# Rotary embedding in a two-layer encoder step: the exchange of halves made by on-chip transfers in place of permutation matmuls

## The chip, the cores and the metric

The kernel runs on one core of a Trainium2 chip. The metric is the device time of one execution in microseconds (us), as the median of the runs. Times inside the execution are read from a profile of one of them; there a time such as "at 110.98" counts from the start of the span.

## The reference

One inference step of a 2-layer encoder over 512 prompt tokens and 32 decode tokens, d_model 1024. Each layer projects the normed input with one wide matrix, feeds four head groups, merges them, and adds an MLP and a gated per-layer embedding. The change touches the rotary embedding only, which five 128-row (or narrower) tiles of a layer go through:

```python
def rope(x, pos):
    half = x.shape[-1] // 2
    ...
    x1, x2 = x[..., :half], x[..., half:]
    return jnp.concatenate([x1 * cos - x2 * sin, x2 * cos + x1 * sin], axis=-1)
...
    q_b = rope(s_q.reshape(b, t, SWA_HEADS, SWA_HEAD_DIM), pos)      # 4 heads x 64
    k_b = rope(s_k.reshape(b, t, SWA_KV_HEADS, SWA_HEAD_DIM), pos)   # 2 heads x 64
    k_pe = rope(m_kr, pos)                                           # 1 x 32
    q_p = rope(m_qr.reshape(b, t, MLA_HEADS, MLA_ROPE_DIM), pos)     # 4 heads x 32
```

## The kernel before

Activations lie feature-major: 128 features on the partitions, 544 tokens (512 + 32) along the row. So the two halves of a head are different partitions, 32 apart for heads of 64 and 16 apart for heads of 32, and the exchange of halves moves whole rows between partitions. The sign of the sine is folded into the table `sin`.

The input projection is worked off as units of 128 output features. The first 15 are, in order: MISC (with the 32 rotary key rows), Q0 Q1 K0 K1 V0 V1 (the delta rule), CKV, SK, SV, QR, SQA, SQB, Z0, Z1. TensorE makes a unit with `product` (L1821): 8 k-tiles, each in three passes, since weights and activations are split in a high part and a rest. For each unit a weight goes through SyncE (load to `raw`, 512 KB), ScalarE (`high`, L928, which first waits for the product two units back), GpSimd (`rest`, L799), and VectorE takes the product out of PSUM (`in_tile`, `evacuate`, L1331 and L1332, which links `freed`).

Between the halves of a product and after it TensorE does other work, listed in `HOOKS`: slot `2 * unit` comes in the middle of the unit, slot `2 * unit + 1` behind it. Every engine runs through the same list in its own `mid_unit`. In the middle of SK, SV, SQA, SQB and Z0 stands a rope item: R_KPE, R_SK, R_QR, R_SQA, R_SQB. In the same slots stand steps of the delta rule: `prep` (n, 0) behind a unit and (n, 1) in the middle of the next, from behind CKV to the middle of QR; then `level` (n, 0) in the middle and (n, 1) behind, from the middle of SQA on. The order inside a `prep` or `level` step matters here:

- `prep` (n, 0) ends on VectorE with L1513, which marks `prep_u`. TensorE's `prep` (n, 1) is 24 + 24 matmuls (L1930); the second 24 wait for that mark. VectorE's part of `prep` (n, 1) is `row_sources` (L1478) and L1519, L1520; TensorE's next row sums (L1957, L1958) wait for them.
- `level` (n, 0): TensorE multiplies three batches into PSUM (`xs_pe`), ScalarE copies them out (L1045, `xs`). `level` (n, 1): TensorE multiplies three batches (`ys_pe`), and its third waits until VectorE has finished the first (L1527, L1529, `td`).

A rope item works so: TensorE's `rotate` multiplies the evacuated tile `xr` by a permutation matrix into the idle PSUM bank (L1923, in `both`), marks `rotated`; VectorE's `finish_rope` multiplies that by the sine (L1364), `xr` by the cosine (L1365), and adds the two to the place where the tile is used. For QR these are four additions (L1380), one per head. TensorE waits for `roped` before the next unit's product, as that takes the bank. VectorE does `finish_rope` in the order of `HOOKS`, ahead of the delta step of its slot. `t1`, the tile named rope in the profile, is VectorE's scratch.

Of the kernel before, what the change touches and what calls it, by code (L numbers as in the profile page):

```python
# [20 lines left out]
ALU = mybir.AluOpType  # L21
# [44 lines left out]
OUTPUTS = O_PLE + 2 * KT  # L66


(K_IDENT, K_TRIBD, K_ONESBD, K_ONES, K_ROT64, K_ROT32) = (i * P for i in range(6))
K_MASK = 6 * P  # L70
K_ISTK = K_MASK + LEVELS * C
K_TRI = K_ISTK + C
K_SEL = K_TRI + C
# [189 lines left out]


R_KPE, R_SK, R_QR, R_SQA, R_SQB = range(5)


def hooks():
# [68 lines left out]
def build(nc, w_units, w_kv, params, consts, x_t, p_t, conv_state, ckv_cache, kpe_cache, k_cache, v_cache,  # L337
          s_state, sconv_state, y_t, gdn_s_p, gdn_s_s, conv_p, conv_s, swa_k_p, swa_k_s, swa_v_p, swa_v_s,
          ckv_p, ckv_s, kpe_p, kpe_s, sconv_p, sconv_s):
    with ExitStack() as ctx:  # L340
# [162 lines left out]
        c_r = signal("c_r", 1)  # L503
        c_done = signal("c_done", 1)
        rope_in = signal("rope_in_s", 4)
        rotated = signal("rotated", 5)
        roped = signal("roped", 5, 1)
        v_raw = signal("v_raw", 1)
        misc_in = signal("misc_in", 1)
# [405 lines left out]
        def _(act):  # L915
# [89 lines left out]
            def inv_rms(l, phase):  # L1005
# [2 lines left out]
                link(act, act.activation(two(rms[:]), pt[:, 0:2, 0:HALF], ACT.Ln, bias=eps, scale=1.0 / D), act_step, l)  # L1008
                mark(act.activation(rms[:], rms[:], ACT.Exp, scale=-0.5), rms_ready)

            def l2_square(l, j):

                act.wait_ge(*silud.at(l, j + 1))
                mark(act.activation(l2_scratch[j], qkv[:, j, 0:TOK], ACT.Square), qk_sq)
# [82 lines left out]

            def mid_unit(l, n):
                for item, *a in HOOKS[n]:
                    if item == "c_square":  # L1100
                        act.wait_ge(*craw.at(l, 1))
                        act.wait_ge(*l2n.at(l, 4))
                        act.activation(sqt[:, 0:SEQ], ckv[:, 0:SEQ], ACT.Square)
                        mark(act.activation(sqt[:, SEQ:TOK], ckv[:, SEQ + PAST:KEYS], ACT.Square), c_sq)
                    elif item == "c":
                        b = 2 - 2 * slot(l, n // 2)
                        act.wait_ge(*c_sum.at(l, 1))
                        link(act, act.activation(two(sqt[:]), pp[:, b:b + 2, 0:HALF], ACT.Ln, bias=eps, scale=1.0 / P),
                             act_step, l)
                        mark(act.activation(sqt[:], sqt[:], ACT.Exp, scale=-0.5), c_r)  # L1110
                    elif item == "l2_square":
                        l2_square(l, *a)
                    elif item == "delta" and a[0] != "gates":
                        step(l, *a)
# [183 lines left out]
        def _(dve):  # L1298
# [55 lines left out]
                a = sq[:, 0:2 * SEQ].rearrange("p (n r t) -> p n r t", r=2, t=C)[:, :, tile, :]  # L1354
                return [(a, slice(0, SEQ)), (sq[:, 2 * SEQ + tile * DEC:2 * SEQ + (tile + 1) * DEC], slice(SEQ, TOK))]

            def finish_rope(l, j, b):

                rows = slice(0, DEC) if j == R_KPE else slice(0, P)
                cos, sin = (cos32, sin32) if j in (R_KPE, R_QR) else (cos64, sin64)  # L1360
                src = misc if j == R_KPE else xr
                dve.wait_ge(*rotated.at(l, j + 1))
                dve.wait_ge(trig.sem, 16 * (l + 1))
                step(dve.tensor_tensor(two(t1[rows, :]), pp[rows, b:b + 2, 0:HALF], two(sin[rows, :]), ALU.mult), l)  # L1364
                step(dve.tensor_tensor(src[rows, :], src[rows, :], cos[rows, :], ALU.mult), l)  # L1365
                if j in (R_SQA, R_SQB):
                    for a, t in swa_q_parts(j - R_SQA):
                        s0, s1 = src[:, t], t1[:, t]
# [306 lines left out]
            def mid_unit(l, n):  # L1675
                for item, *a in HOOKS[n]:
# [7 lines left out]
                    elif item == "c":  # L1684

                        dve.wait_ge(*c_r.at(l, 1))
                        g = par[:, R_CNORM:R_CNORM + 1]
                        dve.scalar_tensor_tensor(ckv[:, 0:SEQ], ckv[:, 0:SEQ], g, sqt[:, 0:SEQ], ALU.mult, ALU.mult)
                        mark(dve.scalar_tensor_tensor(ckv[:, SEQ + PAST:], ckv[:, SEQ + PAST:], g, sqt[:, SEQ:TOK],
                                                      ALU.mult, ALU.mult), c_done)  # L1690
                    elif item == "rope":
                        finish_rope(l, a[0], 2 - 2 * slot(l, n // 2))
                    elif item == "delta":
                        delta(l, *a)

            dve.wait_ge(*gains_in.at(0, 16))
            for m in range(KT - 1):
# [101 lines left out]
        def _(pe):  # L1799
# [130 lines left out]
                    ins = pe.matmul(dst[r, j * C:(j + 1) * C], lhsT(r), rhs(r), start=True, stop=True)  # L1930
                return ins

            def rotate(l, j, b, slot_free):

                rows = slice(0, DEC) if j == R_KPE else slice(0, P)
                wait_apart(pe, slot_free, rope_in.at(l, j) if j else misc_in.at(l, 1))
                perm = k_(K_ROT32 if j in (R_KPE, R_QR) else K_ROT64)[rows, 0:rows.stop]
                mark(both(l, pp[rows, b:b + 2, :], perm, (xr if j else misc)[rows, :]), rotated)

            def step(l, kind, n, s):  # L1940
                n0 = n * BC
                if kind == "gates" and n == 0:
# [149 lines left out]
            def mid_unit(l, n):  # L2092
                b = 2 - 2 * slot(l, n // 2)
                for item, *a in HOOKS[n]:

                    slot_free = freed.at(l, n // 2)
                    if item == "rope":
                        rotate(l, a[0], b, slot_free)
                    elif item == "c":
                        pe.wait_ge(*slot_free)  # L2100
                        pe.wait_ge(*c_sq.at(l, 1))
                        mark(both(l, pp[:, b:b + 2, :], ones, sqt), c_sum)
# [13 lines left out]
            for l in range(DEPTH):  # L2116
                first_units(l)
                assert U_CKV > 1 and U_V0 > 1
                for u in range(2, N_PRE):
                    for item, *a in HOOKS[2 * u - 2]:  # L2120

                        if item == "rope":
                            pe.wait_ge(*roped.at(l, a[0] + 1))
                        elif item == "c":
                            pe.wait_ge(*c_r.at(l, 1))
                    product(l, u, u, ha[l], range(KT), between=lambda: mid_unit(l, 2 * u))
                    mid_unit(l, 2 * u + 1)
# [100 lines left out]
def constants(norm_final):  # L2228
# [7 lines left out]
    c[:, K_TRIBD:K_TRIBD + P] = same & (i <= j)  # L2236
    c[:, K_ONESBD:K_ONESBD + P] = same
    c[:, K_ONES:K_ONES + P] = 1
    c[:, K_ROT64:K_ROT64 + P] = (i ^ 32) == j
    c[:, K_ROT32:K_ROT32 + P] = (i ^ 16) == j  # L2240
    k = np.arange(C)[None, :]
    for lv in range(LEVELS):

# [147 lines left out]
```

## Time and profile before

| what | value |
|---|---|
| time, median of 3 runs | 1542.1 us (1542.02 to 1543.05) |
| profiled execution, its own time | 1542.11 us |
| span of its trace | 1540.3 us (so 1.8 us lie around it) |
| TensorE's granted clock over the span | 0.998 |
| TensorE matmul / weight load busy | 1508.1 us (98%) / 1430.6 us (93%) |
| VectorE / ScalarE / GpSimd busy | 997.4 / 710.2 / 832.9 us |
| mean busy share of the 16 DMA engines, in the slices of the rope items | 0.1 to 0.2 |

Busy shares are averages over the whole span. What the rope items cost must be read from their two stretches, about 72 to 142 us (layer 0) and 830 to 900 us (layer 1). The rows quoted below are of layer 0; layer 1 repeats them 757.98 us later (its R_QR matmuls start at 867.84 against 109.86) within 0.3 us.

### The profile page before, as it was taken

The page shows a single profiled execution, that of the slowest core. Times are in us where ns is not written, and L with a number is a line of the kernel's source. Part 1 is how long each engine was busy: PE and PEld are TensorE (multiplying, and loading weights), DVE is VectorE, ACT ScalarE, POOL GpSimd, SP SyncE. Part 2 cuts the span into 40 slices and gives each one's busy share as a digit, 9 for nine tenths or more (in the row PEclk, how much of TensorE's full clock was granted, in tenths as well). Part 3 has the DMA queues.
Part 4 walks back from the last instruction along what each step waited for, and adds up shares of the span by engine and source line. Part 5 has one row for each costly group of instructions (what it writes and reads, how often), then busy time and mean ns, then how long its engine had stood idle before and what let it go on. Part 6 is the DMA issues. An engine that isn't in the chain of part 4 may idle for free.

```text
span 1540.3 us, 33894 instructions
## 1 busy us (share of the span) xinstructions
PE 1508.1 (98%) x14202; PEld 1430.6 (93%) x14202; DVE 997.4 (65%) x1674; ACT 710.2 (46%) x1280; POOL 832.9 (54%) x468
## 2 busy tenths in 40 slices
PE   7999999999999999999999999999999999999997
PEld 6999888899999999999998998888999999999996
DVE  7865535547848668586688654464487594766955
ACT  6621445535434344445455224464454443434553
POOL 4354112265866849578643541114659476694973
PEclk9999999999999999999999999999999999999999
DMA  6211011332241412322322110214323224142132
GB/s 207 80 46 43 21 53 42 53 131 83 83 137 54 135 59 94 99 69 100 106 79 70 43 44 15 59 46 71 126 80 105 88 81 139 45 135 69 42 96 86
DMA packets 45129, 123.81 MB, mean 80 GB/s; under 512 B 10993, under 2 KB 15857, under 8 KB 44721
## 3 DMA queue, kind: packets, MB, share of 16 engines
q1 hardware_dynamic: 44688, 119.86, 25.8%
q8 instruction: 113, 1.85, 0.5%
q10 hardware_dynamic: 288, 1.78, 0.3%
q14 instruction: 40, 0.32, 0.1%
HBM read 117.86 MB, written 3.76 MB: 79 GB/s over the span
## 4 chain that ended last, share of the span: by engine, by line
PE 82%; DVE 10%; ACT 3%; POOL 2%; issue 2%; DMA 1%; SPq 0%; DVEq 0%; ACTq 0%; POOLq 0%
PE psum_p L1821 39%; PE psum_t L1878 19%; PE psum_p L1894 6%; PE psum_t L1930 6%; DVE conv_out L1350 2%; PE psum_p L2089 2%; PE psum_t L2060 2%; PE psum_p L2069 2%; PE psum_p L1857 1%; POOL w_rest L811 1%; PE psum_t L2053 1%; PE psum_t L1914 1%; PE psum_p L1914 1%; DVE mla_q L1380 1%; PE psum_p L1923 1%
## 5 line engine op out<-in xcount | busy, mean ns | idle before, releaser
L1821 PE MATMUL psum_p<-hidden,w_high 128*128 128x272 f32 x3680 | 619.2, 290 | 2.6 <-POOL w_rest L799 1.1
L1821 PEld LDWEIGHTS psum_p<-hidden,w_high 128*128 128x128 f32 x3680 | 519.8, 188 | 8.4 <-POOL w_rest L799 3.1
L799 POOL TENSOR_TENSOR w_rest<-raw,w_high 128x1024 fp32r<-128x1024 f32 x110 | 268.8, 2447 | 383.7 <-ACT w_high L928 383.7
L1821 PE MATMUL psum_p<-hidden,w_rest 128*128 128x272 f32 x1840 | 379.9, 288 | 0.0
L1821 PEld LDWEIGHTS psum_p<-hidden,w_rest 128*128 128x128 f32 x1840 | 288.4, 188 | 0.0
L811 POOL TENSOR_TENSOR w_rest<-w_sums,w_high 128x512 fp32r<-128x512 f32 x128 | 208.1, 1651 | 93.2 <-DVE w_sums L1603 55.2
L928 ACT ACTIVATE w_high<-raw 128x1024 fp32r<-128x1024 f32 x112 | 117.9, 1055 | 149.6 <-PE psum_p L1821 101.5
L1878 PE MATMUL psum_t<-hidden_split_a,w_high 128*128 128x272 f32 x896 | 178.7, 290 | 2.1 <-issue 1.0
L1878 PE MATMUL psum_t<-hidden_split_b,w_high 128*128 128x272 f32 x896 | 176.9, 288 | 0.4 <-DVE hidden_split_b L1619 0.4
L1878 PEld LDWEIGHTS psum_t<-hidden_split_a,w_high 128*128 128x128 f32 x896 | 140.0, 188 | 5.8 <-issue 4.7
L1878 PEld LDWEIGHTS psum_t<-hidden_split_b,w_high 128*128 128x128 f32 x896 | 140.3, 188 | 0.8 <-DVE hidden_split_b L1619 0.8
L942 ACT ACTIVATE w_high<-w_sums 128x512 fp32r<-128x512 f32 x128 | 79.7, 629 | 113.7 <-DVE w_sums L1601 56.7
L1878 PE MATMUL psum_t<-hidden_split_b,w_rest 128*128 128x272 f32 x448 | 129.0, 288 | 0.0
L1878 PE MATMUL psum_t<-hidden_split_a,w_rest 128*128 128x272 f32 x448 | 128.9, 288 | 0.0
L1629 DVE SCALAR_TENSOR_TENSOR rope_in<-psum_p,rms 128x544 f32<-128x544 f32 x64 | 46.3, 723 | 114.0 <-PE psum_p L1821 101.9
L799 POOL TENSOR_TENSOR w_rest<-raw_more,w_high 128x1024 fp32r<-128x1024 f32 x32 | 80.4, 2521 | 51.4 <-ACT w_high L928 51.4
L973 ACT ACTIVATE hidden_parts<-rope_in 128x544 f32<-128x544 f32 x64 | 42.2, 659 | 122.8 <-DVE rope_in L1629 122.8
L811 POOL TENSOR_TENSOR w_rest<-raw,w_high 128x512 fp32r<-128x512 f32 x48 | 78.9, 1650 | 29.0 <-ACT w_high L942 29.0
L1894 PE MATMUL psum_p<-hidden,w_high 128*128 128x272 f32 x512 | 91.2, 300 | 0.1
L1314 DVE SCALAR_TENSOR_TENSOR hidden<-x,parameters,hidden 128x544 fp32r<-128x544 f32 x48 | 68.3, 1424 | 25.6 <-ACT hidden L997 24.9
L1878 PEld LDWEIGHTS psum_t<-hidden_split_a,w_rest 128*128 128x128 f32 x448 | 84.3, 188 | 0.0
L1878 PEld LDWEIGHTS psum_t<-hidden_split_b,w_rest 128*128 128x128 f32 x448 | 84.3, 188 | 0.0
(307 smaller groups left out, 2627.9 us busy)
## 6 DMA issues: line engine op xcount, KB each, us to landing
raw<-w_units SPq DMA_DIRECT2D x146, 512.0 KB, 3.6
raw_more<-w_units SPq DMA_DIRECT2D x64, 512.0 KB, 3.6
x<-x_t SPq DMA_DIRECT2D x8, 272.0 KB, 6.1
y_t<-y SPq DMA_DIRECT2D x8, 272.0 KB, 2.2
constants<-consts ACTq DMA_DIRECT2D x1, 1088.0 KB, 8.9
ple_in<-p_t SPq DMA_DIRECT2D x2, 544.0 KB, 12.1
constants<-consts SPq DMA_DIRECT2D x1, 1088.0 KB, 5.5
constants<-consts ACTq DMA_DIRECT2D x1, 649.5 KB, 5.6
```

The costliest lines, as they stand in the source:

```text
L799: mark(pool.tensor_tensor(wlo_at(l, s, 2), raw_at(l, u), whi_at(l, s, 2).bitcast(F32), ALU.subtract), lo_done)
L811: mark(pool.tensor_tensor(wlo_at(l, s, 1), src, whi_at(l, s, 1).bitcast(F32), ALU.subtract), lo_done)
L928: mark(act.activation(whi_at(l, place_of(u), 2), raw_at(l, u), ACT.Copy), hi_done)
L942: mark(act.activation(whi_at(l, s, 1), src, ACT.Copy), hi_done)
L973: link(act, act.activation(dst, two(xr[:]), ACT.Square), h_sq, l)
L1314: mark(dve.scalar_tensor_tensor(ha[l][:, m, 1, :], x[:, m, :], g, f(ha[l][:, m, 0, :]), ALU.mult, ALU.subtract), normed)
L1350: step(dve.scalar_tensor_tensor(dst, src[:, j:j + cols], w, dst, ALU.mult, ALU.add), l)
L1629: link(dve, dve.scalar_tensor_tensor(two(xr[:]), psum_of(l, o), 0.0, two(rms[:]), ALU.max, ALU.mult), freed, l)
L1821: ins = pe.matmul(pp[:, 2 * b + h, 0:HALF], w(l, s, 2)[:, cols(k)], rhs[:, k, part, h * HALF:(h + 1) * HALF], start=(n == 0 and z == 0), s ...
L1878: ins = pe.matmul(bank, w(l, s, 1)[:, j * P:(j + 1) * P], hs(l, j)[:, half, part, :], start=(j == 0 and z == 0), stop=(j == PAIRS - 1 and ...
L1894: ins = pe.matmul(pp[:, h, 0:HALF], w(l, s, 2)[:, k * P:(k + 1) * P], ha[l][:, k, half, h * HALF:(h + 1) * HALF], start=(k == 0 and z == 0 ...
L1930: ins = pe.matmul(dst[r, j * C:(j + 1) * C], lhsT(r), rhs(r), start=True, stop=True)
```

## The change

The two permutation matrices go out of the constants, and `rotate` moves from TensorE to ScalarE's queue. There it issues plain transfers from SBUF to SBUF, each with half a head's rows (16 or 32 partitions by 544 words), from the source tile to `t1`: 2 for R_KPE, 4 for R_SK, 8 for R_QR, 4 for R_SQA, 4 for R_SQB, 22 in a layer. `finish_rope` waits for all transfers of its item, multiplies by the cosine, and then `t1` by the sine in place. On VectorE the rope items of a slot now come behind the delta step of that slot. TensorE's wait for `roped` ahead of a product goes.

```diff
-(K_IDENT, K_TRIBD, K_ONESBD, K_ONES, K_ROT64, K_ROT32) = (i * P for i in range(6))
-K_MASK = 6 * P
+(K_IDENT, K_TRIBD, K_ONESBD, K_ONES) = (i * P for i in range(4))
+K_MASK = 4 * P
...
+ROPE_PARTS = (2, 4, 8, 4, 4)
...
-        rotated = signal("rotated", 5)
+        rotated = signal("rotated", 16 * sum(ROPE_PARTS))
...
+            def rotate(l, j):
+
+                src, width, last = (misc, 16, DEC) if j == R_KPE else (xr, 16, P) if j == R_QR else (xr, 32, P)
+                if j == R_KPE:
+                    act.wait_ge(*misc_in.at(l, 1))
+                    act.wait_ge(*l2n.at(l, 4))
+                    act.wait_ge(*craw.at(l, 1))
+                else:
+                    act.wait_ge(*rope_in.at(l, j))
+                for r in range(0, last, 2 * width):
+                    for a, b in ((r, r + width), (r + width, r)):
+                        act.dma_start(t1[a:a + width, :], src[b:b + width, :]).then_inc(rotated.sem, 16)
...
                 for item, *a in HOOKS[n]:
-                    if item == "c_square":
+                    if item == "rope":
+                        rotate(l, a[0])
+                    elif item == "c_square":
...
-            def finish_rope(l, j, b):
+            def finish_rope(l, j):
...
-                dve.wait_ge(*rotated.at(l, j + 1))
                 dve.wait_ge(trig.sem, 16 * (l + 1))
-                step(dve.tensor_tensor(two(t1[rows, :]), pp[rows, b:b + 2, 0:HALF], two(sin[rows, :]), ALU.mult), l)
+                dve.wait_ge(*rotated.at(l, 16 * sum(ROPE_PARTS[:j + 1])))
                 step(dve.tensor_tensor(src[rows, :], src[rows, :], cos[rows, :], ALU.mult), l)
+                step(dve.tensor_tensor(t1[rows, :], t1[rows, :], sin[rows, :], ALU.mult), l)
...
                     elif item == "rope":
-                        finish_rope(l, a[0], 2 - 2 * slot(l, n // 2))
+                        continue
                     elif item == "delta":
                         delta(l, *a)
+                for item, *a in HOOKS[n]:
+                    if item == "rope":
+                        finish_rope(l, a[0])
...
-            def rotate(l, j, b, slot_free):
-
-                rows = slice(0, DEC) if j == R_KPE else slice(0, P)
-                wait_apart(pe, slot_free, rope_in.at(l, j) if j else misc_in.at(l, 1))
-                perm = k_(K_ROT32 if j in (R_KPE, R_QR) else K_ROT64)[rows, 0:rows.stop]
-                mark(both(l, pp[rows, b:b + 2, :], perm, (xr if j else misc)[rows, :]), rotated)
...
-                        if item == "rope":
-                            pe.wait_ge(*roped.at(l, a[0] + 1))
-                        elif item == "c":
+                        if item == "c":
```

## Rows read from the trace of the kernel before

**Rows 1.** The page's chain that ended last, shares of the span by engine.
```profile
PE 82%; DVE 10%; ACT 3%; POOL 2%; issue 2%; DMA 1%; SPq 0%; DVEq 0%; ACTq 0%; POOLq 0%
```

**Rows 2.** The chain of waits from 66 to 140: start, us, what.
```profile
76.32 0.63 DVE qkv L1513 x2
...
76.99 0.92 PE psum_t L1930 x24
...
110.98 0.74 DVE rope L1364
...
118.81 0.56 DVE inverse_t L1529
119.42 1.61 PE psum_t L1930 x48
```

**Rows 3.** Timeline of TensorE, units Z0 and Z1: start, busy us, line, operation.
```profile
134.89 0.77 PE L1821 MATMUL psum_p<-hidden,w_high 128*128 128x272 f32 x4
...
141.27 0.77 PE L1821 MATMUL psum_p<-hidden,w_high 128*128 128x272 f32 x4
...
148.83 0.78 PE L1821 MATMUL psum_p<-hidden,w_high 128*128 128x272 f32 x4
...
154.29 0.78 PE L1821 MATMUL psum_p<-hidden,w_high 128*128 128x272 f32 x4
```

**Rows 4.** Timeline of TensorE in the middle of SK and SV.
```profile
77.84 0.77 PE L1821 MATMUL psum_p<-hidden,w_high 128*128 128x272 f32 x4
...
89.56 0.77 PE L1821 MATMUL psum_p<-hidden,w_high 128*128 128x272 f32 x4
```

**Rows 5.** Timeline of VectorE, SV to SQB; in brackets its idle time before, and the releaser.
```profile
87.84 0.62 DVE L1513 TENSOR_TENSOR qkv<-qkv,level_x 128x192 f32<-128x192 f32 x2
...
93.80 0.85 DVE L1331 TENSOR_TENSOR swa_v<-psum_p,rms 128x272 f32<-128x272 f32 x3
...
95.91 0.56 DVE L1501 TENSOR_TENSOR decay<-psum_t,decay_columns 128x384 f32<-128x384 f32 x1 [1.13 <-PE psum_t L1958]
...
121.55 0.55 DVE L1529 TENSOR_TENSOR inverse_t<-inverse_t,psum_t 128x384 f32<-128x384 f32 x1
```

**Rows 6.** Timeline of ScalarE around SQA's first half.
```profile
106.86 0.49 ACT L1041 ACTIVATE inverse<-psum_t 128x384 f32<-128x384 f32 x1 [0.21 <-PE psum_t L1930]
111.83 0.49 ACT L1045 ACTIVATE level_x<-psum_t 128x384 f32<-128x384 f32 x1 [4.49 <-PE psum_t L1930]
```

**Rows 7.** Timeline of ScalarE and its queue (ACTq) at the start of the kernel.
```profile
13.39 0.38 ACTq L1123 DMA_DIRECT2D constants<-consts  x1
13.80 0.45 ACTq L1124 DMA_DIRECT2D constants<-consts  x1
13.91 0.73 ACT L997 ACTIVATE hidden<-x,parameters 128x544 fp32r<-128x544 f32 x1
```

**Rows 8.** Timeline of SyncE's queue: four issues in a row, and QR's weight load.
```profile
9.55 1.86 SPq L735 DMA_DIRECT2D mla_k<-kpe_cache  x4
...
108.20 0.33 SPq L706 DMA_DIRECT2D raw<-w_units  x1
```

**Rows 9.** DMA issues by line: KB each, median us from issue to landing.
```profile
kpe_p<-mla_kpe SPq DMA_DIRECT2D x2, 64.0 KB, 2.2
...
gdn_s_s<-state SPq DMA_DIRECT2D x2, 64.0 KB, 4.7
parameters<-params SPq DMA_DIRECT2D x2, 31.0 KB, 1.8
```

**Rows 10.** Timelines of VectorE and GpSimd during the four additions of R_QR.
```profile
112.50 1.41 DVE L1380 TENSOR_TENSOR mla_q<-rope_in,rope 32x544 f32<-32x544 f32 x1
...
116.83 0.72 DVE L1380 TENSOR_TENSOR mla_q<-rope_in,rope 32x544 f32<-32x544 f32 x1
...
111.88 1.44 POOL L848 TENSOR_TENSOR factor_t<-lower_t,constants 128x384 f32<-128x384 f32 x1 [0.81 <-PE psum_t L1930]
...
114.74 1.49 POOL L848 TENSOR_TENSOR factor_t<-lower_t,constants 128x384 f32<-128x384 f32 x1
```

More of the change, by code:

```diff
@@ L2096, in mid_unit @@
                     slot_free = freed.at(l, n // 2)
-                    if item == "rope":
-                        rotate(l, a[0], b, slot_free)
-                    elif item == "c":
+                    if item == "c":
                         pe.wait_ge(*slot_free)
@@ L2120, in _ @@
                     for item, *a in HOOKS[2 * u - 2]:
-                        if item == "rope":
-                            pe.wait_ge(*roped.at(l, a[0] + 1))
-                        elif item == "c":
+                        if item == "c":
                             pe.wait_ge(*c_r.at(l, 1))
@@ L2238, in constants @@
     c[:, K_ONES:K_ONES + P] = 1
-    c[:, K_ROT64:K_ROT64 + P] = (i ^ 32) == j
-    c[:, K_ROT32:K_ROT32 + P] = (i ^ 16) == j
     k = np.arange(C)[None, :]
```

## The prediction

> **What bounds the kernel now.** I read the page first: TensorE holds 82% of the chain that ended last and VectorE 10% [rows 1]. The reader is to see a kernel in which a microsecond taken from TensorE counts, but only where no other engine stands right behind it. So the second view is the same chain cut to the stretch of the rope items, 66 to 140. It leaves TensorE at two places that matter here. In the middle of SK it runs through VectorE's L1513 (76.32, ends 76.95) into the second 24 matmuls at 76.99. In SQA it runs through VectorE's rope of QR (from 110.98) and L1529, and comes back to TensorE at 119.42, the third batch of level (1, 1) [rows 2]. At these two places VectorE decides when TensorE goes on. The third view is the timelines of the engines, for the slack at each place.
>
> **What leaves TensorE.** Z0 and Z1 are the same unit with the same level step in the middle, Z0 with the matmuls of a rotation and Z1 without. Z0 takes 141.27 - 134.89 = 6.38 us to its second half, Z1 154.29 - 148.83 = 5.46 [rows 3]. A rotation costs TensorE 0.92 us. If all ten counted, the change would give 9.2 us. One by one:
>
> - R_KPE: without it TensorE would come to the second 24 matmuls some 0.9 us earlier, but L1513 ends at 76.95 all the same, and the chain already runs through it [rows 2]. TensorE waits instead and goes on with the product at 77.84 as before [rows 4]. Gain 0.
> - R_SK: the same pattern one unit on. L1513 ends at 87.84 + 0.62 = 88.46 [rows 5]. In SK the product went on 77.84 - 76.95 = 0.89 after that end, so here at 88.46 + 0.89 = 89.35; before it was 89.56 [rows 4]. Gain 0.21, the rest goes into a wait on L1513.
> - R_SQA, R_SQB: 0.92 each, if the transfers are on time (below).
> - R_QR: decided by VectorE, not by TensorE (below).
>
> **What is added on ScalarE's queue.** 22 transfers a layer. An issue costs the queue 13.80 - 13.39 = 0.41 us by the two that ScalarE makes today, and 1.86 / 4 = 0.46 by four in a row on SyncE [rows 7, 8]. I take 0.46, since these are in a row and small. The ScalarE activation of 13.91 stands in the program ahead of the issue of 13.39 [rows 7]: the queue runs ahead of the engine, so issues lie beside activations already handed over. The time from issue to landing is not to be had for SBUF to SBUF. Rows for 31 to 64 KB go from 1.8 (a load) over 2.2 (a store) to 4.7 (a store behind others) [rows 9]. I take 2.2, the row nearest in size that did not stand behind large loads, and keep 1.8 and 4.7 as bounds.
>
> The Trainium skill, page "DMA: Bandwidth & Descriptors", section "Anatomy of one DMA — SWDGE (gpsimd) path", gives a fixed 2.0 us plus bytes over 436 GB/s (fitted for the other kind of queue). By it the 34 KB parts of QR would land 2.08 us after issue, and the sum would be 0.2 us better. The same page, "Rules for kernel authors", says that below 64 KB a transfer is mostly overhead, which speaks against cutting QR in eight; no row of this trace prices it.
>
> **QR in detail.** ScalarE comes to the rotation behind its three copies of level 0; the last one's wait ended just before 106.86 [rows 6]. With 0.21 gained until then, issues start at 106.65. The last of eight starts 7 x 0.46 later, at 109.87, and lands at 112.1. VectorE began at 110.98 before; so it starts 1.1 us late. It multiplies twice (2 x 0.74) until 113.6. Then four additions. Before, three of them ran beside GpSimd's L848 at about 1.42 us and the last alone at 0.72 [rows 10]. GpSimd's batch waits for TensorE's first batch of level (1, 0), which now comes 0.21 + 0.92 earlier; so it starts about 110.9 rather than 111.88, and its three instructions (the first now alone, about 1.0, then two at 1.45) end near 114.8 and not 116.2. So one addition is slow and three are quick: 113.6 + 1.42 + 3 x 0.75 = 117.3. SQA's `rest` on GpSimd now starts about 116.4 and may slow the last; I add half of 0.7, which gives 117.6. Before, the rope ended at 117.55 and TensorE's third batch started 119.42 - 117.55 = 1.87 us later (evacuation of SQA, then L1527 and L1529). Now: 119.5. TensorE itself would be there at about 118.1 (119.42 less 0.21 + 0.92, and less the 0.2 that it waits there today). So R_QR gives nothing and takes back the 0.21: 0.1 us worse than before at this point. What is late next: behind the issues on ScalarE stand the copies of level (1, 0), before at 111.83 [rows 6], now due from about 110.7. The queue is free at 110.3, so they are not late.
>
> **SQA and SQB.** VectorE evacuates SQA at about the old time, so ScalarE can issue at 118.5. The last of four starts at 119.9 and lands at 122.1. VectorE is busy with `td` until 121.55 + 0.55 = 122.1 [rows 5], so the wait is nothing. Its rope (0.74 + 0.74 + 2.3) must be over when SQB's product is, at about 129.6: 3.7 us of slack for a late landing. SQB is alike. ScalarE's wait for `rope_in` holds back only the next copies, due 5 us later. Gain 2 x 0.92.
>
> **The other places.** For KPE the issues start about 72.9 and land by 76, for SK they start at about 84.8 and land by 88.5; VectorE wants them, now behind its delta step (2.3 us from the ends of L1513 at 76.95 and 88.46), at about 79.2 and 90.8. If that cover went, the rope would hold VectorE's evacuation and the next decay. VectorE's rope of SK then ends near 93.9 as before; SV's evacuation was at 93.80 and had 1.13 us of idle time behind it [rows 5], which shrinks by 0.1 to 0.3. The reordering alone costs nothing: the sum of VectorE's work is the same, and it makes the row sums' inputs earlier. The smaller constants come earlier at the start, where nothing waits for them: 0.
>
> **Sum.** A layer: 0 + 0.21 and then, at SQA's third batch, 0.1 behind the old time instead; then 2 x 0.92. So 1.84 - 0.1 = 1.74, and 3.5 us for two layers. Behind Z1 everything hangs on TensorE or on chains that it starts, so it stays. The profiled execution took 1542.11 us (span 1540.3), the same as the median of 1542.1: forecast 1538.6.
>
> Bounds: with 0.41 per issue and landing after 1.8 QR's transfers land at 111.3, TensorE's third batch starts 0.8 earlier, and a layer gains 2.55: 1537.0. With landing after 4.7 they land at 114.6, 2.5 late; the additions all run quicker or collide with `rest`, so the third batch comes at 121.9, a layer loses 0.6: 1543.3.
>
> **Rivals.**
>
> 1. TensorE's time comes back more fully. If the transfers of QR land by 110.7, the third batch starts when TensorE is ready (118.1), 1.3 us earlier; a layer gains 3.2, in all 1535.8, or 1536.5 with half of it missed. Against it: that landing is under 1 us after the last issue, and no row is under 1.8. Chance 0.11.
> 2. The wait for QR's transfers takes the place of most of the gain. A landing after 3.2 to 4.1 us and not 2.2, between the bounds of [rows 9], beside QR's weight load, issued at 108.20 [rows 8], puts VectorE's start at 113.1 to 114.0. Each microsecond there is one in a layer: 1540.5 to 1542.4, middle 1541.5. For it: the stretch has no slack on VectorE [rows 2]. Chance 0.30.
> 3. Slower: the small transfers stand behind the 512 KB loads on the same DMA engines. From a landing 5.4 us after the last issue, the loss at QR (3.4 a layer) outweighs 2 x 0.92 by more than 1.5, and the time goes over the bound; at 6 us it is about 1545.5. For it: the 4.7 of a store among others [rows 9]. Against: the one load near QR's transfers goes out at 108.20, 1.7 us before the last of them [rows 8], and the next is a unit later. Chance 0.08.
> 4. Transfers of one queue served one after the other at 2.2 each: QR's would land at 124.3, 12 us late in each layer, 1563. Against: four of SyncE's are issued in 1.86 us [rows 8]. Chance 0.03.
>
> **Numbers.** My forecast has 0.48, its own range 1537.8 to 1539.4. This kernel's measurement can tell about 0.2%, 3.1 us, from no change, which puts the bound at 1539.0, inside that range; 0.34 of the 0.48 lie below it. Faster: 0.34 + 0.11 = 0.45. Same: 0.14 + 0.30 = 0.44. Slower: 0.08 + 0.03 = 0.11. The range reaches from the lower bound over rival 2: 1536.8 to 1542.8.
>
> **What the profile after would show.** No L1923 matmul on rope_in or misc. In KPE and SK a wait of TensorE for L1513 in the middle of its 48 matmuls, with the product resumed at 77.8 and about 89.35. On ScalarE's queue 22 issues a layer, 0.41 to 0.46 apart. VectorE's first multiplication of QR about 5.5 us after the first of eight issues, and TensorE's third batch of level (1, 1) waiting for L1529 at about 119.5. Z0's first half and middle in 5.46 and not 6.38. The prediction is wrong if the first multiplication of QR starts before 111 or after 113.5, if VectorE also waits for transfers in SK, SQA or SQB, or if the additions keep 1.42 us.

## The result, and the profile after

The changed kernel takes 1553.18 us (median of 4 runs, 1551.94 to 1553.89) against 1542.22 (1542.02 to 1543.05) for the kernel before on the same chip: a ratio of 1.0067 [1.0055, 1.0079] (in brackets the 95% interval), 11 us slower. 1538.6 was forecast, with a range up to 1542.8. The profiled execution took 1551.94 us, with a span of 1550.1 and a granted clock of 0.995 (before 0.998). The chain of the page, shares by engine, answers to [rows 1]:

```profile
PE 78%; DVE 11%; ACT 3%; POOL 2%; issue 2%; DMA 1%; ACTq 1%; SPq 0%; DVEq 0%; POOLq 0%
```

TensorE has lost four points of the chain; VectorE and the issue queue of ScalarE (ACTq, 0% before) have one more each, and the rest is lost in the rounding. Now the places in the prediction's order, in layer 0. TensorE's timeline in the middle of SK (where KPE's item stands), of SV (SK's item) and of QR, with its idle time and the releaser in brackets (L1949 was L1930, L1840 was L1821, L1529 was L1513):

```profile
76.97 0.92 PE L1949 MATMUL psum_t<-constants,qkv 64*64 64x64 f32 x24 [1.18 <-DVE qkv L1529]
77.82 0.77 PE L1840 MATMUL psum_p<-hidden,w_high 128*128 128x272 f32 x4
...
88.50 0.92 PE L1949 MATMUL psum_t<-constants,qkv 64*64 64x64 f32 x24 [0.50 <-DVE qkv L1529]
89.34 0.77 PE L1840 MATMUL psum_p<-hidden,w_high 128*128 128x272 f32 x4
...
101.99 0.91 PE L1949 MATMUL psum_t<-constants,qkv 64*64 64x64 f32 x24 [1.56 <-DVE qkv L1529]
```

On TensorE, KPE and SK came out as forecast: the waits for L1513's successor, and the product back at 77.82 and 89.34 (forecast 77.8 and 89.35). The third wait, in the middle of the unit QR, was not forecast. VectorE's timeline shows where it starts; beside it, GpSimd's:

```profile
88.48 2.80 DVE L1494 TENSOR_TENSOR level_x<-gates_by_token,constants 128x192 f32<-128x192 f32 x4
...
94.37 2.36 DVE L1390 TENSOR_TENSOR swa_k<-rope_in,rope 128x32 f32<-128x32 f32 x1
96.77 0.85 DVE L1347 TENSOR_TENSOR swa_v<-psum_p,rms 128x272 f32<-128x272 f32 x3
97.66 0.55 DVE L1517 TENSOR_TENSOR decay<-psum_t,decay_columns 128x384 f32<-128x384 f32 x1
```

```profile
88.52 1.17 POOL L842 TENSOR_TENSOR inverse_t<-lower_t,constants 128x384 f32<-128x384 f32 x1 [3.35 <-DVE qkv L1529]
89.77 1.01 POOL L844 TENSOR_TENSOR inverse_t<-constants,inverse_t 128x384 f32<-128x384 f32 x1
93.85 2.83 POOL L800 TENSOR_TENSOR w_rest<-raw,w_high 128x1024 fp32r<-128x1024 f32 x1 [3.06 <-ACT w_high L929]
```

An addition of 128 x 32 took 2.36 us. It was 0.18 before, and it ends as GpSimd's L800 does (94.37 + 2.36 = 96.73; 93.85 + 2.83 = 96.68). The four row sources took 2.80 beside GpSimd's two instructions, 1.17 before. So SV was evacuated at 96.77 and not at 93.80 [rows 5], the 1.13 us of idle time behind it is gone, and the next decay started at 97.66, before at 95.91. The Trainium skill, page "SBUF — State Buffer", section "Who interferes with whom", says that an instruction of VectorE with two inputs in SBUF contends with one of GpSimd that reads SBUF, over a shared port pair that it calls "an exclusive lock". The trace agrees: the 128 x 32 addition, started 0.52 us behind L800, lasted until L800 was over.

Then QR. The chain of waits (start, us, what) has each issue, and the landing behind the last; of the rope's four additions the third:

```profile
108.90 0.03 ACTq L1023
...
108.96 1.61 ACTq L1023
...
110.61 0.61 ACTq L1023
...
113.17 0.61 ACTq L1023
...
113.81 2.03 DMA rope<-rope_in
...
115.93 0.74 DVE rope_in L1380
116.69 0.74 DVE rope L1381
...
118.92 2.77 DVE mla_q L1396
```

Timelines of ScalarE's queue and VectorE:

```profile
108.41 6.00 ACTq L1023 DMA_DIRECT2D rope<-rope_in  x8
```

```profile
115.93 0.73 DVE L1380 TENSOR_TENSOR rope_in<-rope_in,constants 128x544 f32<-128x544 f32 x1 [8.85 <-DMA rope<-rope_in]
...
117.45 4.96 DVE L1396 TENSOR_TENSOR mla_q<-rope_in,rope 32x544 f32<-32x544 f32 x4
```

The landing is what was taken, 2.03. The issuing is not: 6.00 us for eight, 0.64 from one to the next and once 1.6, where 0.46 each was taken, 3.7. VectorE starts 7.5 us after the first issue (forecast 5.5), and the additions still take 4.96 (before 5.05), not the 4.0 of the forecast (3.7, and half of 0.7 for `rest`). Three of them are quick, as forecast; the third runs into GpSimd's `rest` and takes 2.77. In layer 1 the eight issues take 5.00 with no slow one among them, but the last lands 3.38 us after its issue, and VectorE starts 7.9 us after the first. TensorE waits for all this, and then (timeline of TensorE; windows of one us, whose last three columns are the granted clock, the DMA share and GB/s):

```profile
124.29 0.48 PE L1949 MATMUL psum_t<-level_x,inverse_t 64*64 64x64 f32 x4 [4.31 <-DVE inverse_t L1545]
```

```profile
123.00:124.00 1.00, 0.00 (x0) 0.00 (x0) 0.96 (x4) 0.00 (x0) 0.00 (x0) 1.00 0.89 352
124.00:125.00 1.00, 0.71 (x14) 0.71 (x16) 1.00 (x3) 0.00 (x0) 0.00 (x0) 0.54 0.42 115
125.00:126.00 1.00, 1.00 (x24) 1.00 (x23) 0.17 (x1) 0.00 (x0) 0.00 (x0) 0.50 0.54 124
126.00:127.00 1.00, 1.00 (x22) 0.93 (x18) 0.00 (x0) 0.00 (x0) 0.00 (x0) 0.50 0.44 101
127.00:128.00 1.00, 1.00 (x10) 0.95 (x7) 0.83 (x2) 0.00 (x0) 0.00 (x0) 0.76 0.00 0
```

After 4.31 us without a matmul the granted clock is 0.50, the 1.2 GHz level, while TensorE works again. The third batch takes 127.05 - 124.29 = 2.76 us, before 120.96 - 119.42 = 1.54. In layer 1 the wait is 4.66 and the clock stays at 0.50 from 886 to about 892.

**Where the 11 us are.** TensorE's delay against before, in layer 0: +1.55 in QR's unit, +4.87 at the third batch, +6.09 behind it (127.05 against 120.96), then back by one rotation each at SQA and SQB: +5.36 at Z0's start, +4.44 at Z0's second half. The gains of SQA and SQB are real (Z0 takes 145.71 - 140.25 = 5.46 to its second half, 6.38 in [rows 3]). Layer 1 starts 3.9 late, is 9.1 late at its third batch and 9.8 at the end of its rope stretch, which is the whole difference of the spans. Of each layer's delay, 1.40 and 2.45 us arise after the third batch has started, while the clock is low: the batch and the product behind it take 2.76 + 5.64 us in layer 0 and 2.75 + 6.70 in layer 1, against 1.54 + 5.46 with the clock at 1.00.

### The profile page after: what moved, and what is told of

It is laid out like the page before. It is cut to its first block, busy times and chain, and to the rows that moved or that the text cites. A ratio compares the mean times of both kernels' runs of the same rounds, so it can differ in the third digit from the quotient of the medians.

```text
span 1550.1 us, 33850 instructions
## 1 busy us (share of the span) xinstructions
PE 1504.0 (97%) x14162; PEld 1429.7 (92%) x14162; DVE 1001.6 (65%) x1674; ACT 711.1 (46%) x1280; POOL 830.6 (54%) x468
## 4 chain that ended last, share of the span: by engine, by line
PE 78%; DVE 11%; ACT 3%; POOL 2%; issue 2%; DMA 1%; ACTq 1%; SPq 0%; DVEq 0%; POOLq 0%
PE psum_p L1840 37%; PE psum_t L1897 18%; PE psum_p L1913 6%; PE psum_t L1949 6%; DVE conv_out L1366 2%; POOL w_rest L812 2%; PE psum_p L2101 2%; PE psum_p L2081 2%; PE psum_t L2072 2%; PE psum_p L1876 2%; PE psum_t L2065 1%; PE psum_t L1933 1%; PE psum_p L1933 1%; DMA raw<-w_units 1%; ACTq L1023 1%
## 5 line engine op out<-in xcount | busy, mean ns | idle before, releaser
L1840 PE MATMUL psum_p<-hidden,w_high 128*128 128x272 f32 x3680 | 620.2, 290 | 2.5 <-POOL w_rest L800 1.1
L1840 PEld LDWEIGHTS psum_p<-hidden,w_high 128*128 128x128 f32 x3680 | 520.9, 188 | 8.3 <-POOL w_rest L800 3.0
L800 POOL TENSOR_TENSOR w_rest<-raw,w_high 128x1024 fp32r<-128x1024 f32 x110 | 272.0, 2476 | 387.2 <-ACT w_high L929 387.2
L1840 PE MATMUL psum_p<-hidden,w_rest 128*128 128x272 f32 x1840 | 380.2, 288 | 0.0
L1840 PEld LDWEIGHTS psum_p<-hidden,w_rest 128*128 128x128 f32 x1840 | 288.9, 188 | 0.0
L943 ACT ACTIVATE w_high<-w_sums 128x512 fp32r<-128x512 f32 x128 | 79.9, 630 | 113.5 <-DVE w_sums L1617 56.6
L800 POOL TENSOR_TENSOR w_rest<-raw_more,w_high 128x1024 fp32r<-128x1024 f32 x32 | 80.4, 2519 | 51.5 <-ACT w_high L929 51.5
```

Of the source, the lines that this page charges most:

```text
L800: mark(pool.tensor_tensor(wlo_at(l, s, 2), raw_at(l, u), whi_at(l, s, 2).bitcast(F32), ALU.subtract), lo_done)
L943: mark(act.activation(whi_at(l, s, 1), src, ACT.Copy), hi_done)
L1840: ins = pe.matmul(pp[:, 2 * b + h, 0:HALF], w(l, s, 2)[:, cols(k)], rhs[:, k, part, h * HALF:(h + 1) * HALF], start=(n == 0 and z == 0), s ...
```

## The experiments

Times are medians; each ratio is to the kernel before on the same chip. Experiments 1 to 5 ask which part costs what, 6 to 10 what QR's wait is made of, 11 what is worth keeping. From one profile to the next the stretch begins up to 2 us earlier or later (SK's product starts at 71.70 before, at 73.66 in experiment 7); "counted from the start of its stretch" means from that row.

**1. The change with the old order.** VectorE does `finish_rope` ahead of the delta step again.

```diff
                     elif item == "rope":
-                        continue
+                        finish_rope(l, a[0])
                     elif item == "delta":
                         delta(l, *a)
-                for item, *a in HOOKS[n]:
-                    if item == "rope":
-                        finish_rope(l, a[0])
```

> The changed kernel with VectorE's rope items put back ahead of the delta step of their slot; the transfers stay. Theory A (three causes add up in each layer: the new order makes VectorE's row sources and last addition of R_SK run beside GpSimd and costs 1.55 us; R_QR's eight issues of 0.61 to 1.6 us on ScalarE's queue hold VectorE; TensorE's long wait for it drops its clock): L1494's row sources fall from 2.79 back to about 1.17, TensorE resumes in QR at about 101.1 and not 102.83, R_QR's rope starts near 114.2 and not 115.93, and the time falls by 1.7 us a layer to about 1549.8. Theory B (the transfers alone are the loss; the order only moves slack of VectorE about): 1553, since VectorE waits for QR's transfers anyway.

1552.37 us, 1.0068 [1.0052, 1.0085]: as slow as the change; theory A had 1549.8. In layer 0 the row sources are back at 1.17 and the small addition at 0.18, but VectorE, now with the rope first, waits for SK's transfers, and TensorE's row sums behind it wait 0.8 us in layer 0 and 3.5 in layer 1. VectorE's timeline:

```profile
90.03 1.50 DVE L1380 TENSOR_TENSOR rope_in<-rope_in,constants 128x544 f32<-128x544 f32 x1 [1.25 <-DMA rope<-rope_in]
```

In layer 1 one of SK's issues takes 1.28 us and the last lands 3.66 after its issue, so the rope starts 6.3 us after the first issue and not 4.9. That puts the row sources beside GpSimd's `rest`. Timelines of VectorE, GpSimd and TensorE, and a window behind the wait:

```profile
855.21 3.31 DVE L1494 TENSOR_TENSOR level_x<-gates_by_token,constants 128x192 f32<-128x192 f32 x4
```

```profile
855.65 2.38 POOL L800 TENSOR_TENSOR w_rest<-raw,w_high 128x1024 fp32r<-128x1024 f32 x1 [3.24 <-ACT w_high L929]
```

```profile
859.50 0.91 PE L1966 MATMUL psum_t<-level_x,constants 128*128 128x384 f32 x2 [3.54 <-DVE k_decayed L1536]
```

```profile
860.00:861.00 1.00, 1.00 (x5) 0.60 (x4) 0.40 (x3) 0.00 (x0) 0.00 (x0) 1.00 0.88 356
```

So with transfers for SK either order loses, each in its own way. The granted clock stayed at 1.00 behind this wait of 3.54 us.

**2. The order alone.** The kernel before, its matmuls kept, with VectorE's rope items behind the delta step.

> The kernel before with nothing but the new order on VectorE (rope behind the delta step); TensorE still multiplies by the permutations. Theory A: 1.5 to 1.9 us lost in each layer at the middle of QR, not given back later: 1545.3 to 1546.0. Theory B: 1542.2, no change.

1545.69 us, 1.0025 [1.0015, 1.0035]. The same collisions without any transfer:

```profile
88.72 2.80 DVE L1478 TENSOR_TENSOR level_x<-gates_by_token,constants 128x192 f32<-128x192 f32 x4
...
94.62 2.33 DVE L1374 TENSOR_TENSOR swa_k<-rope_in,rope 128x32 f32<-128x32 f32 x1
```

The order costs 3.6 us; level (1, 0) starts 1.75 later in layer 0 (112.62 against 110.87) and 3.27 in layer 1, which itself begins 1.74 late. Here 0.9 us of it is TensorE's wait for `roped` ahead of QR's product, which the change does not have; in the change the same lateness reaches TensorE as the wait in the middle of QR.

**3. QR alone.** The kernel before, in its old order, with QR's eight transfers on ScalarE's queue; the other four rotations stay on TensorE.

```diff
+MOVED = (R_QR,)
...
                     if item == "rope":
-                        rotate(l, a[0], b, slot_free)
+                        if a[0] in ON_PE:
+                            rotate(l, a[0], b, slot_free)
```

> The kernel before with R_QR alone moved by eight transfers on ScalarE's queue; all other rotations on TensorE and the old order. If the causes add: the change cost 11.0, of it the new order 3.5 (measured alone), R_SQA and R_SQB -2.9 (measured alone), R_KPE and R_SK about -0.4, so QR alone must cost about 10.8: 1553. By the parts read from the trace (3.4 us of waiting a layer and 1.2 to 2.3 us of low clock): 9.2 to 11.4, that is 1551.3 to 1553.5. A rival, that the loss at QR comes only behind the late VectorE that the new order leaves: under 1546.

1552.53 us, 1.0063 [1.0048, 1.0078]: 10.2 slower. The timelines of VectorE and TensorE, and windows behind them:

```profile
113.74 0.76 DVE L1385 TENSOR_TENSOR rope_in<-rope_in,constants 128x544 f32<-128x544 f32 x1 [8.24 <-DMA rope<-rope_in]
```

```profile
122.21 0.48 PE L1955 MATMUL psum_t<-level_x,inverse_t 64*64 64x64 f32 x4 [3.81 <-DVE inverse_t L1554]
...
124.96 1.27 PE L1846 MATMUL psum_p<-hidden,w_high 128*128 128x272 f32 x4
```

```profile
123.00:124.00 1.00, 1.00 (x25) 1.00 (x24) 0.09 (x1) 0.00 (x0) 0.00 (x0) 0.50 0.00 0
...
126.00:127.00 1.00, 1.00 (x7) 1.00 (x6) 0.10 (x1) 0.00 (x0) 0.00 (x0) 0.50 0.00 0
```

This is the cleanest account of QR. VectorE's rope starts at 113.74 and not 110.98, +2.76; the third batch at 122.21 and not 119.42, +2.79; the product behind it at 124.96 and not 120.96, +4.00, since the batch runs at half the clock (2.75 us for 1.54); the next product at 132.34 and not 127.34, +5.00, since the half product between runs at the low clock too. Of 5 us in this layer, 2.8 are the wait and 2.2 the clock. Layer 1 loses 5.6: the wait is 4.04, and the low clock costs 2.55.

**4. SQA and SQB alone.** The same edit with `MOVED = (R_SQA, R_SQB)`.

> The kernel before with only R_SQA and R_SQB moved by transfers from ScalarE's queue; R_KPE, R_SK and R_QR stay on TensorE and VectorE's order is the old one. Theory A: each of the four rotations gives its full 0.92 us, as VectorE has slack there: 1538.5. Theory B or C (transfers slow the stretch wherever they stand): 1542 or more.

1539.17 us (10 runs), 0.9979 [0.9970, 0.9989]: faster than both kernels. From level (1, 0) to the end of the rope stretch a layer takes 1.76 and 1.74 less than before (150.77 - 111.36 = 39.41 against 41.17 in layer 0), nearly 2 x 0.92. SQA's transfers land later than forecast (122.1), but at this place VectorE had been idle before as well, waiting for TensorE's rotation. VectorE's timeline of this run, then of the kernel before (this run's stretch starts 0.48 later):

```profile
125.71 0.73 DVE L1385 TENSOR_TENSOR rope_in<-rope_in,constants 128x544 f32<-128x544 f32 x1 [3.06 <-DMA rope<-rope_in]
```

```profile
125.20 0.72 DVE L1364 TENSOR_TENSOR rope<-psum_p,constants 128x544 f32<-128x544 f32 x1 [3.10 <-PE psum_p L1923]
```

The parts add up: 3.6 + 10.2 - 2.9 = 10.9, measured 11.0. KPE and SK are left out of this sum, and the next experiment shows that such sums do not hold in general, so the agreement is in part luck.

**5. All but QR.** `MOVED = (R_KPE, R_SK, R_SQA, R_SQB)`, old order.

> The kernel before, with its old order, and KPE, SK, SQA and SQB moved to transfers; QR stays on TensorE. Theory A (parts add up): the change in the old order took 10.3 us, QR alone 10.2, SQA and SQB alone -2.9, so KPE and SK in the old order cost 3.0, by VectorE's wait for SK's transfers, and this kernel comes out at 1542.2 (1541 to 1543.5). Rival B, QR's wait and SK's are one and the same loss (what SK's delays is waited for again at QR's): without QR the cost of SK is hidden in slack, and the time is that of SQA and SQB alone, 1539.2 (1538.5 to 1540).

1540.71 us, 0.9990 [0.9980, 0.9999]. It lies between the two theories: KPE and SK together cost 1.5 us beside SQA and SQB (1540.71 - 1539.17), half of what adding up asked for. VectorE waits 1.75 us for SK's transfers (its row at 90.47) and TensorE's row sums 0.8 in both layers; the 3.5 of layer 1 in experiment 1 are not there, as the rope starts 5.4 and 5.5 us after SK's first issue and the row sources, at 1.17, are done about when GpSimd's `rest` starts. Whether they meet hangs on less than a microsecond in the transfers; why those of SK took longer in experiment 1 stays open.

**6. One transfer in place of eight.** Experiment 3 with a single transfer of 16 rows for QR; the other 112 rows of its exchange are left out.

> The kernel before with only QR taken from TensorE, as in the run of QR alone, but a single transfer of 16 rows in place of eight: the other 112 rows of QR's exchange are left out, and everything else (the forms of VectorE's two multiplications, the additions, the old order) stays. Theory A, the loss is the time that QR's eight transfers take: one is issued in about 0.5 us at 106.8 and lands 2.0 to 2.1 later (the landing seen after QR's last issue), so the rotation can start at about 109.5, before TensorE's result let it (110.98), and the 10.2 us of QR alone are gone: 1541 to 1543, TensorE's wait for the third batch at most 1.5, its granted clock at 1.00. Rival B, the loss comes from VectorE's changed operations or from the removal on TensorE itself, whatever the transfers take: over 1547. Rival C, a landing has its own wait of several us whatever the count: rotation still after 113, 1550 or more.

1541.80 us (10 runs), 0.9997 [0.9988, 1.0007]: the 10.2 us are gone. The chain of waits, and TensorE's timeline:

```profile
108.57 2.40 DMA rope<-rope_in
...
111.06 1.36 DVE rope_in L1385
```

```profile
120.79 0.33 PE L1955 MATMUL psum_t<-level_x,inverse_t 64*64 64x64 f32 x4 [0.40 <-DVE inverse_t L1554]
```

(In this profile the stretch starts 1.7 us late: VectorE's evacuation ahead of QR is at 106.38 and not 104.68.) TensorE waits 0.4 us, and the clock is 1.00 over 118 to 122. Neither VectorE's changed operations nor the removal on TensorE cost anything by themselves; the time that eight transfers take does. The run also shows how little QR can give in this order, however short the transfers. Its rope starts at 111.06, 1.6 us earlier than before counted from the start of its stretch, but then it runs beside GpSimd's batch (its two multiplications take 1.35 and 1.40, 0.72 each before), and the third batch comes only 0.34 earlier.

**7. Four transfers of 32 rows.** The change with `ROPE_PARTS = (2, 4, 4, 4, 4)`; QR's halves are exchanged 32 rows apart, which is not QR's rotation, but moves the same bytes.

> The changed kernel with R_QR moved in four transfers of 32 rows, as R_SQA is, in place of eight of 16 (the same bytes; it exchanges halves of 64 there, so that part of the computation is another one). Theory A (the number of issues on the queue counts): the issues take 2.4 us and not 5.0 to 6.0, the rope of QR starts 3 us earlier, TensorE's wait there falls from 4.3 to about 1.3 us, its clock stays at the upper level, and a layer wins 3 + 1.2 to 2.3 us: 1543.5 to 1545. Theory C (bytes or the landing of small rows on the DMA engines count, not the issues): the rope of QR starts at 115.9 as before and the time stays at 1553.

1551.83 us, 1.0062 [1.0047, 1.0077]. The issues take half as long, 3.22 us, yet VectorE starts 6.53 us after the first (7.52 in the change) and TensorE still waits 3.8 in both layers. It was to be 1543.5 to 1545. What is saved in issuing comes back in landing: the last of four lands 3.84 us after its issue (4.42 in layer 1), where the last of eight took 2.03 (3.38).

**8. Z1's load held back.** SyncE issues Z1's 512 KB weight load only when QR's transfers have landed; once with eight transfers, once with the four of experiment 7.

```diff
                 for u in range(3, N_IN - 2):
+                    if u == U_Z1:
+                        sp.wait_ge(*rotated.at(l, 16 * sum(ROPE_PARTS[:R_QR + 1])))
```

> The changed kernel, with SyncE's load of Z1's weight held until R_QR's transfers have landed. Before this edit that load went out at about 109.7, in the midst of the eight issues. Theory D (the small transfers collide with the 512 KB load twice: one issue waits 1.6 us for it, and rows that go out ahead of it or beside it land up to 2 us late): eight issues at an even 0.61 us, VectorE's rope of QR 6.9 us after the first issue or less (now 7.5 and 7.9), 0.6 to 1.0 us earlier in a layer, with a shorter spell of low clock: 1550 to 1552. Theory A (the number of issues alone): no change, 1553. Holding the load itself costs nothing, its use is 15 us away.

> The run with QR moved in four transfers of 32 rows (halves of 64 exchanged there), and Z1's load held until they have landed. Theory D: the four issues take 2.4 us and the last lands 2.0 us after its issue, so VectorE's rope starts 3.9 us after the first issue (6.5 without the hold), TensorE's wait falls from 3.8 to about 1.1 us, its clock stays up, and the time falls to 1544 to 1546. Theory C (what counts is not the load but the bytes or the rows of the transfer): 6.5 us and 1552 stay.

With eight: 1552.90 us, 1.0069 [1.0054, 1.0084], nothing gained. VectorE's rope starts 7.1 us after the first issue and 7.7 in layer 1 (7.5 and 7.9 in the change); in layer 1 the eight issues take 5.00 us and the last lands 3.25 after its issue, almost as with the load beside them (5.00 and 3.38). So the load is not what makes the change slow. With four: 1550.04 us, 1.0049 [1.0034, 1.0064]. Here holding the load helps: the last transfer lands 2.08 and 2.09 us after its issue, 3.84 and 4.42 in experiment 7, and the rope starts 4.8 and 4.0 us after the first issue, 6.5 and 6.3 there. In layer 1 that is at 875.19, 3.7 us earlier than with eight (878.17, in a stretch that starts 0.7 earlier). TensorE's third batch gains 1.5 of it. The chain of waits of layer 1, and GpSimd's timeline:

```profile
873.00 2.09 DMA rope<-rope_in
...
875.99 1.41 DVE rope L1383
...
881.03 2.93 DVE mla_q L1398
...
885.83 2.83 PE psum_t L1951 x48
```

```profile
872.44 7.27 POOL L851 TENSOR_TENSOR factor_t<-lower_t,constants 128x384 f32<-128x384 f32 x6
881.02 2.35 POOL L802 TENSOR_TENSOR w_rest<-raw,w_high 128x1024 fp32r<-128x1024 f32 x1 [1.31 <-ACT w_high L931]
```

The last addition starts 0.01 us behind GpSimd's `rest` and takes 2.93 us, where one undisturbed takes 0.72. The four take 6.53 together (4.98 with eight transfers), and a multiplication takes 1.41 (0.73) beside GpSimd's batch. So 2.2 of the 3.7 us won on the transfers are lost to GpSimd, TensorE still waits 3.1 us, and the clock still falls.

**9. QR's transfers from SyncE.** The change with QR's eight issued by SyncE, ahead of Z1's load.

> The changed kernel with R_QR's eight transfers issued by SyncE ahead of its load of Z1's weight, as soon as the tile is there, in place of by ScalarE behind its three copies. Theory D: the issues start at about 107.1 and not 108.4, none waits for the load, the rope starts at about 113.5 and not 115.9, TensorE waits about 1.9 us and keeps its clock: 2.4 us and 1.2 to 2.3 us saved in a layer, 1545 to 1547. Theory E (issues of such transfers cost more on any queue while another queue loads): 1550 or more.

1550.71 us, 1.0050 [1.0033, 1.0066]: at most 2.5 better than the change, where 1545 to 1547 was expected. The queue starts with the data, but its issues cost the same, 0.59, and one of them 1.51; TensorE still waits 3.8 and 3.5. The chain of waits:

```profile
110.40 0.59 SPq L751
111.04 1.51 SPq L751
112.58 0.59 SPq L751
...
114.48 2.00 DMA rope<-rope_in
```

**10. Two queues at once.** Experiment 3 with rows 0 to 63 issued by ScalarE, rows 64 to 127 by SyncE.

> The kernel before with only QR moved to transfers, in the old order, but its eight transfers split between two queues: ScalarE issues those of rows 0 to 63, SyncE those of rows 64 to 127, ahead of Z1's weight load. Theory A, the wait is made of the issuing (0.6 us for each, one behind the other, one of them 1.6) and a landing of 2.0 to 2.1 behind the last: both queues begin at 106.8, their last issues end at 109.3 to 110.3, the rotation can start at 111.3 to 112.4 in place of 113.7, TensorE's wait for the third batch shrinks to 1.5 to 2.5 from 3.8, and the granted clock falls little or not at all: 1543.5 to 1547. Rival B, the transfers themselves are what takes time (the queues' work is served one after the other, or each issue waits for a common part): rotation still at 113 or later, 1551 or more.

1550.99 us, 1.0058 [1.0041, 1.0075]. Theory A is missed too: both queues are done early (SyncE's by 108.8, ScalarE's by 110.3), but the rope starts at 113.40, 0.3 us earlier than in experiment 3 (1.4 in layer 1, counted from the start of its stretch), and TensorE waits 3.8 and 3.5. What is saved in issuing comes back in landing; the last transfer waited for:

```profile
109.67 3.64 DMA rope<-rope_in
```

The Trainium skill, page "DMA: Bandwidth & Descriptors", section "Issuing engines are not separate DMA queues", says that issuing on several engines saves only their sequencers' time, as the transfers run on the same DMA engines; this run agrees. The load of 512 KB had been issued at 108.87 and stood beside these transfers; whether it or the eight themselves make up the 3.64 was not separated.

**11. KPE, SQA and SQB.** `MOVED = (R_KPE, R_SQA, R_SQB)`, old order.

> The kernel before with KPE, SQA and SQB moved to transfers, in the old order; SK and QR stay on TensorE. Theory A: KPE's rotation on TensorE ended with VectorE's wait, not with work of its own, and its two transfers land before VectorE asks for them, so it gives nothing and costs nothing beside SQA and SQB: 1539.2 (1538.6 to 1539.8). Rival B, its transfers are waited for by VectorE ahead of the decay columns: 1540.5 or more. Rival C, the stretch freed on TensorE is time at the unit of SK: 1537.5.

1539.03 us (10 runs), 0.9979 [0.9970, 0.9988]: the same as without KPE. KPE on transfers is free and worth nothing, so the 1.5 us of experiment 5 are SK's. This and experiment 4 are the best versions, 2.9 to 3.3 us under the kernel before.

## Why the prediction was wrong

- **A rotation costs TensorE 0.92, and SQA and SQB give it back twice a layer: right.** Experiment 4 has 1.75 in each rope stretch for 1.84. Its time fell by 2.9 in all, not 3.5; the rest lies outside the stretches and was not traced.
- **KPE 0 and SK 0.21 on TensorE: right** to 0.02 us at both places. But SK's 0.21 is gone by the middle of QR.
- **"The reordering alone costs nothing": wrong, 3.6 us by itself** (experiment 2). The reason given was that the sum of VectorE's work stays. The sum did not stay: instructions moved under GpSimd's, and a 0.18 became 2.36. The rows that carry the warning were in the prediction [rows 10], where they priced QR's additions (1.42 beside GpSimd, 0.72 alone), and were not asked for the moved items.
- **QR "gives nothing and takes back the 0.21": the step that failed.** It was added up from four terms, here for layer 0. The start: issues from 108.41 and not 106.65, 1.8 late, by the reordering. The issuing: priced with 0.46 each, from rows of loads; they are 0.64 apart, and one took 1.6, so the last starts 5.40 us after the first and not 3.22, 2.2 more. The landing: 2.03 for 2.2, right, but 3.38 in layer 1. The additions: one slow and three quick, as forecast, but the slow one meets `rest` and takes 2.77, so 4.96 for 4.0, 1.0 more. Together the third batch came at 124.29 and not at 119.5. The path was right (VectorE decides when the third batch starts), and so all 4.8 us reached TensorE; the sizes of start, issuing and additions were not.
- **The granted clock was in no term.** With a wait of 3.1 to 4.8 us in TensorE at the third batch come some 3 to 7 us at or near 0.50, in both layers of the change and of experiments 1, 3 and 7 to 10, at a cost of 1.2 to 2.6 us each time; the granted clock is 1.00 over the same stretches of both layers in experiments 2, 4, 5, 6 and 11, which have no such wait. By experiment 3 it makes 2.2 of 5.0 us in layer 0. That the low clock follows from the wait is read from these pairs; no run kept the wait and filled it with matmuls. The length of the wait does not decide it alone: behind the 3.54 us at the row sums in layer 1 of experiment 1 the clock stayed at 1.00. Before that wait TensorE had run 1.6 us of 64 x 64 matmuls behind a product, before the others 3.0 us of them.
- **Rival 2 named the right place** (the wait for QR's transfers), but at one for one. In experiment 3 VectorE starts 2.76 late, and the layer is 5.00 later. **Rival 1** (a third batch 1.3 us earlier, if the landing allows it) does not hold: in experiment 6 the landing allowed it and the batch came 0.34 earlier. **Rival 3** (small transfers behind the 512 KB loads) had the right sign; but experiment 8 holds the load back and changes nothing with eight transfers. With four it is right: there the load delays the landing by about 2 us.
- **Two of the prediction's own signs of being wrong came true.** QR's first multiplication started at 115.93, after 113.5, and in layer 1 VectorE waited 2.36 us for SQB's transfers (at 907.03), though TensorE lost nothing by that.

## What to carry to other kernels

Price a moved dependency by its whole latency and by the slack at its place, not by the work it takes off: the same 0.92 us was won twice a layer where VectorE had been idle for 3 us anyway (SQA, SQB), and its removal cost 5 us a layer where the next matmuls hung on the result (QR). Before instructions are reordered or started earlier on VectorE, lay GpSimd's timeline beside it: here, two-input additions that started behind a long GpSimd instruction lasted until it was over. And a new wait of 3 us or more in TensorE can cost more than its length, here 1.2 to 2.6 us more at each of the 16 waits before the third batch, as the clock behind it is low, and nothing at the one before the row sums.

## What the runs showed of the hardware

- Transfers from SBUF to SBUF of 34 or 68 KB (16 or 32 rows of 544 words) keep the issuing queue busy for 0.51 to 0.61 each and follow each other at 0.55 to 0.64 us, on ScalarE's and SyncE's queue alike. In every series of four or eight for QR in layer 0 one took 0.9 to 1.6; in layer 1 those of ScalarE alone went without (5.00 for eight, 2.44 for four). What makes the slow one stays open: it came with the load held back, too (1.22 and 1.41, experiment 8).
- Most land 1.9 to 2.1 us after issue where no load is beside them; in the change the median of QR's sixteen is 2.9 and the longest of all takes 4.9. With the load held back QR's median is 2.0, but in layer 1 the last of eight still takes 3.25 (experiment 8).
- A VectorE addition of 128 x 32 took 0.18 us alone and 2.33 to 2.36 beside GpSimd's 128 x 1024 subtraction.
